# Query scales kept out of the queries in two cross attentions, and three row norms summed up by GpSimd

## What is computed

```python
def rmsnorm(x, g):
    y = xf * lax.rsqrt(jnp.mean(xf * xf, axis=-1, keepdims=True) + EPS)
    return y * g

def cross_attn(h, mem_n, wq, wkv, wo, q_norm, k_norm):      # 4 heads of 128
    q = rmsnorm((h @ wq).reshape(bsz, s, X_HEADS, X_HD), q_norm)
    k, v = split_cols(mem_n @ wkv, (X_INNER, X_INNER))
    k = rmsnorm(k.reshape(bsz, MEM_LEN, X_HEADS, X_HD), k_norm)
    sc = jnp.einsum('bshd,bmhd->bhsm', q, k) * (X_HD ** -0.5)
    p = jax.nn.softmax(sc, axis=-1)
    return jnp.einsum('bhsm,bmhd->bshd', p, v).reshape(bsz, s, X_INNER) @ wo

for l in range(DEPTH):
    x = x + mixer(rmsnorm(x, norm_mix[l]))
    x = x + cross_attn(rmsnorm(x, norm_cross[l]), rmsnorm(mem, norm_mem[l]), ...)
    x = x + conv_ffn(rmsnorm(x, norm_ffn[l]), ...)
```

## Time and profile before

| what | us |
|---|---|
| median of 3 runs (2726.71 to 2733.36) | 2729.97 |
| the profiled execution | 2732.31 |
| its span from first to last instruction | 2730.5 |
| PE busy in the span | 2625.6 |
| DVE busy | 1765.6 |
| ACT busy | 1131.3 |
| POOL busy | 10.0 |

### The profile page before, as it was taken

One profiled execution on the slowest core, in us unless ns is written; L12 is line 12 of the kernel. 1 busy time (PEld: TensorE's weight loads), 2 busy tenths in 40 slices (PEclk: granted clock), 3 DMA queues, 4 the chain that ended last, 5 costly groups with the idle time before them and its releaser, 6 DMA issues.

```text
span 2730.5 us, 46605 instructions
## 1 busy us (share of the span) xinstructions
PE 2625.6 (96%) x18448; PEld 2434.1 (89%) x18448; DVE 1765.6 (65%) x2499; ACT 1131.3 (41%) x1470; POOL 10.0 (0%) x18
## 2 busy tenths in 40 slices
PE   6898998999899999999999999999899999999999
PEld 5898898899898899889988988899788998899889
DVE  4666666665777764776477666765777647764774
ACT  2434444343444443444344344444444434443443
POOL 0000000000000000000000000000000000000000
PEclk8899999999999999999999999999999999999999
DMA  5343443345445565556555543345256655566554
GB/s 153 101 124 101 116 117 102 123 155 170 147 145 187 185 191 180 182 186 191 180 182 187 169 149 108 109 132 165 90 185 192 192 183 181 186 190 183 181 188 150
DMA packets 429635, 432.64 MB, mean 158 GB/s; under 512 B 15487, under 2 KB 427796, under 8 KB 429108
## 3 DMA queue, kind: packets, MB, share of 16 engines
q1 hardware_dynamic: 422832, 422.63, 50.3%
q0 software_dynamic: 1584, 5.40, 0.7%
q10 hardware_dynamic: 5076, 2.56, 0.3%
HBM read 428.44 MB, written 2.10 MB: 158 GB/s over the span
## 4 chain that ended last, share of the span: by engine, by line
PE 85%; DVE 8%; ACT 3%; issue 2%; DMA 1%; SPq 0%; POOL 0%; ACTq 0%; DVEq 0%
PE stream L1537 24%; PE stream L1522 13%; PE stream L1524 13%; PE stream L1523 13%; PE stream L1538 12%; PE bank L1616 1%; PE bank L1557 1%; DVE w_lo L904 1%; ACT scores L838 1%; PE bank L1506 1%; ACT w_hi L492 1%; PE stream L1616 1%; DMA cst<-in_consts 1%; DMA stage<-in_mem 1%; DVE v_buf L958 0%
## 5 line engine op out<-in xcount | busy, mean ns | idle before, releaser
L904 DVE TENSOR_TENSOR w_lo<-w_raw,w_hi 128x1024 fp32r<-128x1024 f32 x800 | 966.0, 1222 | 587.7 <-ACT w_hi L492 583.9
L492 ACT CAST w_hi<-w_raw 128x1024 fp32r<-128x1024 f32 x800 | 835.6, 1048 | 832.9 <-PE stream L1524 481.9
L1537 PE MATMUL stream<-h,w_hi 128*128 128x512 f32 x2816 | 992.2, 398 | 0.0
L1538 PE MATMUL stream<-h,w_lo 128*128 128x256 f32 x2816 | 788.9, 280 | 0.0
L1537 PEld LDWEIGHTS stream<-h,w_hi 128*128 128x128 f32 x2816 | 528.9, 188 | 130.3
L1522 PE MATMUL stream<-act,w_hi 128*128 128x256 f32 x2016 | 577.5, 286 | 1.0 <-DVE act L931 1.0
L1524 PE MATMUL stream<-act,w_lo 128*128 128x256 f32 x2016 | 570.7, 283 | 0.0
L1523 PE MATMUL stream<-act,w_hi 128*128 128x256 f32 x2016 | 570.5, 283 | 0.0
L1538 PEld LDWEIGHTS stream<-h,w_lo 128*128 128x128 f32 x2816 | 531.4, 189 | 0.1
L1522 PE MATMUL stream<-h,w_hi 128*128 128x256 f32 x1536 | 462.2, 301 | 3.1 <-DVE w_lo L904 3.1
L1523 PE MATMUL stream<-h,w_hi 128*128 128x256 f32 x1536 | 440.6, 287 | 0.0
(11 more groups left out here) (356 smaller groups left out, 1728.0 us busy)
## 6 DMA issues: line engine op xcount, KB each, us to landing
w_raw<-in_ffn_in_w SPq DMA_DIRECT2D x352, 512.0 KB, 4.5
w_raw<-in_ffn_out_w SPq DMA_DIRECT2D x176, 512.0 KB, 3.9
w_raw<-in_hyb_in_w SPq DMA_DIRECT2D x96, 512.0 KB, 3.9
w_raw<-in_swa_in_w SPq DMA_DIRECT2D x48, 512.0 KB, 3.6
w_raw<-in_xkv_w SPq DMA_DIRECT2D x32, 512.0 KB, 3.4
w_raw<-in_hyb_out_w SPq DMA_DIRECT2D x32, 512.0 KB, 3.5
w_raw<-in_swa_out_w SPq DMA_DIRECT2D x32, 512.0 KB, 3.5
w_raw<-in_xq_w SPq DMA_DIRECT2D x16, 512.0 KB, 3.6
```

What stands on the lines that cost most here:

```text
L492: nc.scalar.copy(whi[:, k], raw[:, n % NRAW]).then_inc(hi_split, 1)
L904: v.tensor_tensor(wlo[:, k], raw[:, n % NRAW], whi[:, k].bitcast(F32), ALU.subtract).then_inc(lo_split, 1)
L1537: mm(bank[:, m, :], whi[:, k, kk, w], h[:, kt, :, :], start=(q == 0 and kk == 0), stop=False, skip_group_check=True)
L1538: last = mm(bank[:, m, 0:TOK], wlo[:, k, kk, w], h[:, kt, 0, :], start=False, stop=(q == 3 and kk == len(kts) - 1), skip_group_check=True)
```

## The change

Two things are changed.

**Row norms.** In the stages `mix0`, `ffn0` and `mix1`, GpSimd adds the squares of groups 0 to 6 into `sacc` (which is the buffer `norm_r`), six additions of 128x512 for each norm. PE multiplies by ones twice instead of eight times: `sacc` at group 6 and the last square at group 7. ACT's squares now wait for GpSimd's additions where they waited for PE. The additions of `mix0` stand in GpSimd's queue between the loads of the first and the second quarter of layer 1's memory, those of `ffn0` after the last quarter and ahead of the positions, those of `mix1` at the end.

```diff
+            def add_squares(name):
+                phase, turn = S_PHASE[name], POOLED.index(name)
+                pool.wait_ge(ss_done, ss_total(phase - 1))
+                for g in range(1, 7):
+                    pool.wait_ge(sq_ready, 8 * phase + g + 1)
+                    if g == 1:
+                        nc.gpsimd.tensor_tensor(sacc[:], xsq[:, 0], xsq[:, 1], ALU.add).then_inc(sq_added, 1)
+                    else:
+                        pool.wait_ge(sq_added, 6 * turn + g - 1)
+                        nc.gpsimd.tensor_tensor(sacc[:], sacc[:], xsq[:, g % 2], ALU.add).then_inc(sq_added, 1)
+            load_mem(0, range(4))
+            load_mem(1, range(1))
+            add_squares("mix0")
+            load_mem(1, range(1, 4))
+            add_squares("ffn0")
             pool.wait_ge(pieces_done, SWKV)
 ...
+            add_squares("mix1")
 # square (ACT)
+                if g >= 2 and name in POOLED:
+                    act.wait_ge(sq_added, 6 * POOLED.index(name) + max(g - 2, 1))
 # sum_squares (PE)
+                if name in POOLED:
+                    if g == 6:
+                        pe.wait_ge(rstd_ready, phase)
+                        pe.wait_ge(sq_added, 6 * POOLED.index(name) + 6)
+                        for b in range(2):
+                            mm(bank[:, 0:TOK], ones, sacc[:, b * TOK:b * TOK + TOK], start=(b == 0), stop=False, skip_group_check=True)
+                    if g == 7:
+                        pe.wait_ge(sq_ready, 8 * phase + 8)
+                        for b in range(2):
+                            last = mm(bank[:, 0:TOK], ones, sq[:, 1, b * TOK:b * TOK + TOK], start=False, stop=(b == 1), skip_group_check=True)
+                        last.then_inc(ss_done, 1)
+                    return
```

```diff
 # exps (ACT)
-                        last = f(xp[...], B[2 + h % 2][...], ACT.Exp, scale=X_HD ** -0.5, bias=..., accum_out=...)
+                        last = f(xp[...], x_scores(layer, h)[...], ACT.Exp, scale=xrq[:, 2 * h + u:2 * h + u + 1], bias=..., accum_out=...)
 # scale (ACT)
+                    link(f(xrq_log[:, cols4], xq_sums(layer, j), ACT.Ln, bias=eps_col, scale=1.0 / X_HD))
+                    f(xrq[:, cols4], xrq_log[:, cols4], ACT.Exp, scale=-0.5).then_inc(n_r, 1)
 # scale (DVE)
+                    dve.wait_ge(n_r, ni + 1)
+                    link(refine(xrq[:, cols4], xrq_log[:, cols4], xq_sums(layer, j), X_HD))
+                    v.tensor_scalar(neg_xrq[:, cols4], xrq[:, cols4], -(X_HD ** -0.5), None, ALU.mult)
+                    v.tensor_scalar(xrq[:, cols4], xrq[:, cols4], X_HD ** -0.5, None, ALU.mult).then_inc(n_out, 1)
 # common (DVE), stage XQ
-                        evac_scaled(two(nraw[:]), 0, GROUP[XQ[layer]] + t // 4, XQ[layer] + t)
-                    if t == 5:
-                        head_norm(ni, nraw, nr, nsq, HB, xq[:, 0:2, :], "xq_norm", layer)
-                    if layer and t == 6:
+                        evac_scaled(xq[:, t // 4 * 2:t // 4 * 2 + 2, :], 0, GROUP[XQ[layer]] + t // 4, XQ[layer] + t)
+                    if t == 4:
+                        scale(0)
+                    if layer and t == 4:
                         negmax(0)
                         negmax(1)
-                    if layer and t == 7:
+                    if layer and t == 6:
                         norm(0)
+                        norm(1)
 # common (DVE), layer 1 behind the last piece
-                    norm(1)
+                    scale(1)
+                    negmax(2)
+                    negmax(3)
                     outp(0)
-                    head_norm(ni + 1, nraw, nr, nsq, HB, xq[:, 2:4, :], "xq_norm", layer)
-                    negmax(2)
                     outp(1)
-                    negmax(3)
                     norm(2)
                     norm(3)
 # sums (PE)
+                            last = mm(xq_sums(layer, j)[:, k:k + 1], nsq[:, o:o + P], ones[:, 0:1], start=True, stop=True)
 # common (PE)
                     if t == 4:
-                        head_ss(ni, nsq, HB)
-                    if layer and t == 6:
+                        sums(0)
+                    if layer and t == 4:
                         scores(0)
                         scores(1)
 # common (PE), layer 1 behind the last piece
-                    head_ss(ni + 1, nsq, HB)
+                    sums(1)
+                    scores(2)
+                    scores(3)
+                    turn(1)
                     pv(0)
-                    turn(1)
-                    scores(2)
                     pv(1)
-                    scores(3)
                     turn(2)
                     pv(2)
```

More of the change, by code:

```diff
@@ L86 @@
 S_PHASE = {"x": 0, "mem0": 1, "mix0": 2, "xo0": 3, "ffn0": 4, "mix1": 5, "xo1": 6}
+POOLED = ("mix0", "ffn0", "mix1")
 N_MEM = [0, 4]
@@ L456, in _, with load_mem @@
             pool.wait_ge(ba_split, 1)
[L458 removed]
+            def load_mem(layer, quarters):
                 mv = a["mem"].rearrange("b (t p) d -> p (b t) d", p=P)
[L460 removed]
+                for j in quarters:
                     if layer or j:
@@ L1301, in common @@
                 ni = N_XQ[layer]
-                HB = B[1 if layer else 5]
-                negmax, norm, outp = cross(layer)
+                negmax, norm, outp, scale = cross(layer)
                 for t in range(8):
@@ L1834, in common @@
                 sum_squares(mix, 7, xsq, B[0])
-                ni = N_XQ[layer]
-                HB = B[1 if layer else 5]
-                scores, turn, pv = cross(layer)
+                scores, turn, pv, sums = cross(layer)
                 for t in range(8):
```

100 lines of the change are left out of this document (65 added, 35 removed).

## The result

The changed kernel takes 2711.94 us (median of 5 runs, 2710.54 to 2718.92), the kernel before 2732.56 us beside it (5 runs, 2726.71 to 2736.57): ratio 0.9929 [0.9914, 0.9943], so 19.4 us less by the ratio (15.6 to 23.5 by its interval). The forecast was 22.2 us less and 2707.8 us.

A forecast was written before the change was run, and what follows sets the result against it. PE was taken as the bound, busy 2625.6 of 2730.5 us. The terms -14.2 + 0.2 - 1.0 - 5.9 - 1.3 = -22.2 us, from 2730.0, gave 2707.8 us, with a range of 2702 to 2718.

The forecast's parts named there:

- Step 1: Three row norms: 18 sums of 0.86 us leave PE, less a 0.44 us stop at group 6 each; net -14.2 us.
- Both reasons for the small stop: Norms, group 6: an addition takes 0.69 to 1.23 us of 1.33 us cover, and waits only for DVE's running L941; 0.44 us.
- Step 2: Attention sums as columns: four 128x1 matmuls cost PE about what one 128x512 did; +0.2 us in all.
- Step 3: Layer 1's XQ stage: scores(0) no longer waits for xq, needing only the group's evacuation; -1.0 us.
- Step 4: Layer 1's tail, last piece to XO: a shorter chain takes 17.3 us instead of 23.2; -5.9 us (-3.9 to -7.5).
- I take 1.6: Layer 1's tail: time lost to the lower clock, added to the 15.7 us full-clock chain; 1.6 us, between 0 and 3.5.
- Step 5: Layer 0's quarters: PE's 3.35 us wait for h goes, a load is late next; -1.3 us (0 to -2).
- The additions come late: Norms: GpSimd waits out DVE's row of two-input instructions, PE stalls up to 6.3 us in all; 2712.8 us, chance 0.15.
- The tail gives less: Layer 1's tail: lower clock (+1.9 us) and outp(0) behind both negmax (2 us) leave 2 us; 2711.7 us, chance 0.15.
- The sums were not the bound: Norms: loads could not follow a faster stream, so the 14.2 us go and 2722 is left; chance 0.04.
- Slower: Norms: GpSimd additions of some 9 us or more make PE wait and the change lose; about 2740 us possible, chance 0.03.

The follow-up runs named there:

- add_series: The changed kernel with 20 more GpSimd additions of 128x512 on constants, back to back beside layer 0's MLP, nobody waiting for them; 2728.83 us in one execution.
- cross_only: The changed kernel with all sums of squares back on PE, keeping only the new cross attentions; ratio 0.9970 to the kernel before.
- norm2_first: The changed kernel with one line moved: DVE does norm(2) ahead of outp(1) in layer 1's tail; ratio 0.9908 to the kernel before.
- changed_again: The changed kernel, untouched, measured once more in another set of runs; ratio 0.9926 to the kernel before.
- all_three: norm2_late plus matmuls nobody reads (fillers) in PE's waits, in layer 1's tail and layer 0's quarters; 2703.94 us, ratio 0.9887 to the kernel before.
- norm2_late: The changed kernel with PE taking GpSimd's total at group 7 and norm(2) ahead of outp(1) on DVE; 2698.68 us, ratio 0.9876 to the kernel before.
- late_sum_again: Second run, on another chip, of the changed kernel with PE taking GpSimd's total at group 7 instead of 6; ratio 0.9907 to the kernel before.
- sums_only: The kernel before with only GpSimd's additions for the norms, the cross attentions unchanged; ratio 0.9948 to the kernel before.

## Why the forecast held, and where it was off

**Step 1, fewer sums: right, and nearly to the number.** Six intervals of 12.38 us became 11.52, so a sum is 0.86 us as read from the earlier trace rows, and all of it was on PE's path: 15.5 us. The stop at group 6 is 0.55 us where I took 0.44, so the net is 13.8 and not 14.2. Both reasons for the small stop were half right. The addition was dearer than my upper end (1.27 us at the shortest, in add_series), and the times fit an addition that lets a running L985 pass. What I left out is the other direction: GpSimd holds DVE. Here it cost nothing, since no PE wait for `w_lo` appeared in the norms; in add_series it cost 8.6 us or more.

**Step 2, sums as columns: right.** L1875 takes 0.95 to 1.05 us for four narrow matmuls, as L1949 did. ACT's Ln and Exp take 0.26 and 0.21 us on 128x4, and DVE's five operations some 0.20 from start to start.

**Step 3, the first scores of layer 1: right.** There is no wait ahead of `scores(0)` and `turn(0)`; the first two of the earlier trace rows are gone. From the last square of mix1 to the start of the last matmul of XQ it is 27.18 us where it was 28.13, so 0.95 us of the 1.0 forecast.

**Step 4, the tail: the chain right, the clock mis-sized.** 15.4 us at full clock against 15.7. From the start of XQ's last matmul to XO's first it is 19.0 us in after and 23.6 in before: 4.6 us less, where 5.9 were forecast. PE did wait for `outp(0)` ahead of `pv(1)`, 1.07 us. In after it wasn't the two `negmax` that held `outp(0)`: DVE stood idle for 0.85 us until `pv(0)` came, since the scores took 3.22 us at the lower clock. Where the scores ran at full clock (cross_only, norm2_first) it was as forecast: DVE goes from `negmax(3)` to `outp(0)` without a wait, and PE's wait is 1.07 us as well. Nor was it the longest wait. That was `turn(2)` for `norm(2)` behind `outp(1)`, a link that my own list had and that I didn't name as late. The term that failed is "I take 1.6": the tail lost 3.5 us to the clock, at the upper end of my 0 to 3.5, and XO 2.0 us more. I had let the clock's effect end with the tail. With the first scores the stretch gave 3.5 us and 2.7 in the repeat, of 6.9, and 5.2 us in the means of all executions. The upper end of my 0 to 3.5 makes the lower end of the gain 23.2 - 19.2 = 4.0 us, not the 3.9 that I wrote.

**Step 5, the quarters of layer 0: the mechanism right, the gain given back.** The wait for `h` went and the load was late next, 2.41 us against 2.3 forecast. From quarter 0 to quarter 3 it is 721.54 - 703.52 = 18.0 us, where it was 20.0. But the granted clock over the quarters is 0.92, and over the same stretch of before 0.96, and only 0.45 us was left (1.24 in changed_again, 0.7 in the means). With PE kept at full clock by fillers, all_three had 1.4 us less than norm2_late, but no less than late_sum_again without them, so that the clock took the gain back is likely and not shown.

**The sum.** -13.8 - 0.45 - 3.5 = -17.8 us by the stretches, against -22.2. Of the 4.4 us that are missing 0.4 is the stop, 0.75 layer 0 and 3.3 layer 1, where the clock took 1.9 + 2.0 = 3.9 us more than I had allowed it. That is the account of one pair of executions. In the means of all it is 13.8 + 0.7 + 5.2 = 19.7 us, and 2.5 us are missing instead of 4.4.

**The rivals.** *The additions come late* fell: the wait was 0.32 and not 1.6 to 2.1 us; GpSimd needs only a gap between two of DVE's instructions, and then holds the second. I had taken from the Trainium skill's page SBUF — State Buffer, section Who interferes with whom, only that GpSimd has to wait; its rule holds both ways. *The tail gives less* came nearest: layer 1 gave 3.5 and 2.7 us, where the forecast had 6.9. This rival's own working, 3.9 us less, leaves 3.0 and not the 2 that I wrote: 2 is what is left of the tail. Its time, 2711.7 us, is the measured 2711.94, in part by luck: beside it the kernel before took 2732.56 us and not the 2730.0 from which I counted, and in the means layer 1 gave 5.2. Its first cause, the clock, was at work. Its second, `outp(0)` behind both `negmax`, was there where the scores ran at full clock, but cost nothing beyond my chain, which had that link and came out at 15.4 us; the rest was the clock in XO. *The sums were not the bound* fell to sums_only. *Slower* was far off, at 1.58 us for the addition; and add_series shows that its path would have been another one, through DVE and the split of the weights, not through PE's wait for GpSimd.

**Left open:** why the unchanged stretches take one of two lengths 3.4 us apart (757.0 or 760.5 us behind the last square, 689.6 or 693.0 us to ffn0, with the old order of the attention as with the new), why the one ahead of mix1 lies anywhere from 250.8 to 254.7 us, what decides how much of the tail runs at the lower clock, and with them the 5 us between norm2_late and all_three.

## What to carry to other kernels

Where PE is the bound, work taken from its full stretches was worth its start-to-start time to the digit here; a shorter chain in an idle stretch gave less than its length in the profiles, since the granted clock fell around the pauses and the bill ran on into the full stretch behind it. So cut the pauses first, by moving the one small operation that the next PE step waits for ahead of those that nobody needs yet, which here was one moved line and 44.61 us for 51.7 in the mean, with the doubt about `scores(2)` above. And an addition on GpSimd beside DVE's two-input instructions has to be charged to DVE as well: harmless once in a group of 9 us, 8.6 us or more lost with twenty back to back.

## What the runs showed of the hardware

- The lower clock outlasts the pauses. XO's dense matmuls ran 4.6 us at one L1574 every 0.64 us instead of 0.36 behind the tail, and the same code took 47.97 us from square to square at a granted clock of 0.96 and 53.06 at 0.84.
- An addition of 128x512 in float32 on GpSimd is 1.27 us at the shortest and 1.58 beside DVE's L985; of 128x256, 1.03 us beside the same. DVE's addition of 128x512 is 0.69.
- A two-input instruction of DVE that starts behind an addition of GpSimd takes over 1 us more: L985 1.54 us instead of 0.48, `w_lo` 2.30 instead of 1.22.
- ACT's exponential of 128x256 with a scale that comes as a column takes 0.56 us, with a constant scale 0.47. These rows are after's and before's:

```profile
L743 ACT ACTIVATE x_probs<-bank,x_max,log1p 128x256 f32<-128x256 f32 x16 | 8.8, 562 | 2.8 <-DVE x_max L1278 2.8
```

```profile
L706 ACT ACTIVATE x_probs<-bank,x_max 128x256 f32<-128x256 f32 x16 | 7.4, 470 | 15.4 <-DVE x_max L1231 15.4
```
